# GDN triangular inverse on TensorE: its first four levels as 32 by 32 blocks at four places of the array

## The reference, cut to what matters

```python
lower = jnp.where(strict, jnp.einsum('bhtd,bhsd->bhts', kb, kc) * decay, 0.0)
sol = lax.linalg.triangular_solve(eye + lower, rhs, left_side=True, lower=True, unit_diagonal=True)
u, w = sol[..., :dv], sol[..., dv:]
v_new = u - jnp.einsum('bhcd,bhde->bhce', w, S)
```

## Time and profile before

| what | value |
|---|---|
| median of 3 runs | 1388.18 us (1387.21 to 1388.41) |
| the profiled execution's own time | 1389.42 us |
| its span, first to last instruction | 1387.5 us |
| what lies around the span | 1.92 us |
| PE busy | 1371.8 us, 99% |
| DVE, ACT, POOL busy | 62%, 42%, 25% |
| mean granted TensorE clock | 0.995 |

### The profile page before, as it was taken

One profiled execution on the slowest core, in us unless ns is written; L12 is line 12 of the kernel. 1 busy time (PEld: TensorE's weight loads), 2 busy tenths in 40 slices (PEclk: granted clock), 3 DMA queues, 4 the chain that ended last, 5 costly groups with the idle time before them and its releaser, 6 DMA issues.

```text
span 1387.5 us, 27546 instructions
## 1 busy us (share of the span) xinstructions
PE 1371.8 (99%) x10726; PEld 1335.5 (96%) x10726; DVE 854.1 (62%) x1425; ACT 584.1 (42%) x1061; POOL 352.9 (25%) x478
## 2 busy tenths in 40 slices
PE   8999999999999999999999999999999999999998
PEld 8999999999889999999999999998999799999998
DVE  6666646467676666655766655567663667666542
ACT  6333323434765333332433332367644544333331
POOL 4000013876426000012100002466766340000000
PEclk9999999999999999999999999999999999999999
DMA  7655962334522655854455594143332325555661
GB/s 202 182 148 149 275 173 55 117 115 136 160 69 66 174 148 147 223 159 103 122 151 151 151 251 132 43 121 92 93 93 78 97 82 145 151 151 157 165 163 38
DMA packets 324068, 188.35 MB, mean 136 GB/s; under 512 B 10986, under 2 KB 321384, under 8 KB 323996
## 3 DMA queue, kind: packets, MB, share of 16 engines
q1 hardware_dynamic: 322416, 183.23, 48.2%
q0 software_dynamic: 1216, 3.98, 0.9%
q10 hardware_dynamic: 364, 0.15, 0.1%
HBM read 183.22 MB, written 4.11 MB: 135 GB/s over the span
## 4 chain that ended last, share of the span: by engine, by line
PE 94%; DVE 3%; ACT 2%; issue 1%; DMA 0%; POOL 0%; SPq 0%; DVEq 0%; ACTq 0%
PE PS L677 22%; PE PS L678 22%; PE PS L679 22%; PE PS L794 3%; PE PS L815 2%; PE PS L796 2%; PE PS L795 2%; PE PS L817 2%; PE PS L816 2%; PE PS L767 1%; PE PS L769 1%; PE PS L768 1%; DVE h_lo L2019 1%; PE PS L1258 1%; PE PS L1277 1%; PE PS L1290 1%
## 5 line engine op out<-in xcount | busy, mean ns | idle before, releaser
L677 PE MATMUL PS<-h_hi,w_parts 128*128 128x320 f32 x1408 | 436.6, 310 | 1.8 <-DVE h_lo L2019 1.1
L679 PE MATMUL PS<-h_hi,w_parts 128*128 128x320 f32 x1408 | 435.1, 309 | 0.0
L678 PE MATMUL PS<-h_lo,w_parts 128*128 128x320 f32 x1408 | 435.0, 309 | 0.0
L677 PEld LDWEIGHTS PS<-h_hi,w_parts 128*128 128x128 f32 x1408 | 264.3, 188 | 3.4 <-DVE h_lo L2019 1.7
L678 PEld LDWEIGHTS PS<-h_lo,w_parts 128*128 128x128 f32 x1408 | 264.3, 188 | 0.3
L679 PEld LDWEIGHTS PS<-h_hi,w_parts 128*128 128x128 f32 x1408 | 264.3, 188 | 0.0
L1434 ACT ACTIVATE w_parts<-gu 128x1024 fp32r<-128x1024 f32 (+1 forms) x178 | 176.9, 1041 | 159.8 <-PE PS L679 155.0
L677 PE MATMUL PS<-act_hi,w_parts 128*128 128x320 f32 x704 | 217.7, 309 | 0.0
L679 PE MATMUL PS<-act_hi,w_parts 128*128 128x320 f32 x704 | 217.5, 309 | 0.0
L678 PE MATMUL PS<-act_lo,w_parts 128*128 128x320 f32 x704 | 217.5, 309 | 0.0
L2007 DVE TENSOR_TENSOR w_parts<-gu,w_parts 128x1024 fp32r<-128x1024 f32 x174 | 206.8, 1230 | 4.1 <-ACT w_parts L1434 3.8
(11 more groups left out here) (379 smaller groups left out, 2186.6 us busy)
## 6 DMA issues: line engine op xcount, KB each, us to landing
dn<-in_ffn_w_down SPq DMA_DIRECT2D x32, 1408.0 KB, 7.0
gu<-in_ffn_w_gate SPq DMA_DIRECT2D x87, 512.0 KB, 4.0
gu<-in_ffn_w_up SPq DMA_DIRECT2D x87, 512.0 KB, 5.2
gu<-in_od_w_in SPq DMA_DIRECT2D x32, 512.0 KB, 4.9
gu<-in_ev_w_in SPq DMA_DIRECT2D x26, 512.0 KB, 4.6
dn<-in_ev_w_out SPq DMA_DIRECT2D x4, 1024.0 KB, 5.7
dn<-in_od_w_out SPq DMA_DIRECT2D x4, 1024.0 KB, 5.5
RB<-bias_rows POOLq DMA_DIRECT2D x2, 576.0 KB, 6.1
```

The costliest lines, as they stand in the source:

```text
L677: mm(out, w_hi, hi, start=first, stop=False)
L678: mm(out, w_hi, lo, start=False, stop=False)
L679: return mm(out, w_lo, hi, start=False, stop=last)
```

## The change

The parts y, t and turn of m = 0 to 19 are computed on the 32 by 32 diagonal blocks alone: each of the 4 pairs in 4 blocks of 32 partitions, at four diagonal places of the array, 16 matmuls of 32 by 32 in place of 8 of 64 by 64. The evacuations still read the whole bank regions, so two new memsets on DVE put zeros into banks 4 and 6, with a new semaphore `zeroed`: the first in DVE's step 8, behind `differences(1)`; the second in step 14, behind `first_t(4)`, where it waits for `kt_evac`. `inverse_y(0)` waits for the first, `inverse_t(0)` for the second in place of `kt_evac`. For m = 20 to 24 nothing changes.

```diff
@@ inverse_y, inverse_t, inverse_turn (TensorE)
+            def diagonal_blocks():
+
+                for p in range(C_PAIRS):
+                    for i in range(4):
+                        yield p, slice(32 * i, 32 * i + 32), slice(i % 2 * 32, i % 2 * 32 + 32)
+
             def inverse_y(m):
 
                 c = m % NCH
+                if m == 0:
+                    pe.wait_ge(o["zeroed"], 1)
...
+                if m < 4 * NCH:
+                    for p, rows, w in diagonal_blocks():
+                        ins = mm(by_head(4)[rows, p, w], level[rows, c, p, w], uT[rows, c, p, w], start=True, stop=True)
+                    ins.then_inc(o["y_pe"], 1)
+                    return
...
                 if m:
                     pe.wait_ge(o["t_upd"], m)
                 else:
-                    pe.wait_ge(o["kt_evac"], NCH)
+                    pe.wait_ge(o["zeroed"], 2)
+                if m < 4 * NCH:
+                    for p, rows, w in diagonal_blocks():
+                        ins = mm(by_head(6)[rows, p, w], yT[rows, m % 2, p, w], tT[rows, c, p, w], start=True, stop=True)
+                    ins.then_inc(o["t_pe"], 1)
+                    return
                 for p in range(C_PAIRS):
                     for par in range(2):
                         h = head_rows(par)
-                        left, right = yT[h, m % 2, p, :], tT[h, c, p, :]
-                        if m >= 4 * NCH:
-                            left, right = right, left
-                        ins = mm(by_head(6)[h, p, :], left, right, start=True, stop=True)
+                        ins = mm(by_head(6)[h, p, :], tT[h, c, p, :], yT[h, m % 2, p, :], start=True, stop=True)
...
-                for p in range(C_PAIRS):
-                    for par in range(2):
-                        h = head_rows(par)
-                        ins = mm(by_head(7)[h, p, :], tT[h, m % NCH, p, :], ident[h, h], start=True, stop=True)
+                for p, rows, w in diagonal_blocks():
+                    ins = mm(by_head(7)[rows, p, w], tT[rows, m % NCH, p, w], ident[rows, rows], start=True, stop=True)
                 ins.then_inc(o["u_pe"], 1)
@@ odd (VectorE)
                     if t == 8:
                         differences(1)
+                        ve.wait_ge(o["row_used"], 2)
+                        ve.memset(bank(4)[:, 0:C_PAIRS * CH], 0.0).then_inc(o["zeroed"], 1)
...
                     if 10 <= t < 15:
                         first_t(t - 10)
+                    if t == 14:
+                        ve.wait_ge(o["kt_evac"], NCH)
+                        ve.memset(bank(6)[:, 0:C_PAIRS * CH], 0.0).then_inc(o["zeroed"], 1)
                     if 14 <= t < N_CONV:
                         inverse_update(t - 14)
```

More of the change, by code:

```diff
@@ L517, in build @@
                  "sq qt_pe recip rstd am lev0 kk_pe kk_used kt_evac vt_pe vt_evac t1 u1_pe u1_evac bm y_pe y_evac "
-                 "t_pe u_pe t_upd u_upd cs_pe cs_evac eg qe ks_pe r_ready vn_pe vn_evac o_pe s_pe s_upd osum "
+                 "zeroed t_pe u_pe t_upd u_upd cs_pe cs_evac eg qe ks_pe r_ready vn_pe vn_evac o_pe s_pe s_upd osum "
                  "orecip o_evac decayed turned zt og")
```

## The result

The changed kernel takes 1392.56 us (median of 7 runs, 1390.65 to 1395.61), the kernel before 1388.08 in the same comparison (7 runs, 1387.21 to 1388.41): ratio 1.0033, 95% interval 1.0024 to 1.0043, slower by 0.3%. That is inside the predicted range of 1391 to 1414, on the predicted side, and half of the predicted growth (+4.5 in place of +9.0). The terms of the sum came out otherwise than predicted.

A forecast was written before the change was run, and what follows sets the result against it. PE, busy 99% of the span, was taken to bound the kernel. Terms 3.3 + 1.0 + 3.2 + 1.5 = 9.0 us gave 1398.4 for the profiled execution, 1397.2 us against the median of 1388.18; range 1391 to 1414.

The forecast's parts named there:

- Parts 1 and 2: In y, t and turn: 32 by 32 matmuls, +3.3 us, and nine new array-shape switches between 64 and 32 blocks, +1.0.
- Part 3: In step 14 PE stalls at t(0), waiting for the second memset behind DVE's other work: +3.2 us.
- Part 4: Behind the stall at t(0) PE's clock falls to half, which lengthens the following projection: +1.5 us.
- Part 5: First memset, evacuations and the fetch of 1920 more PE instructions, all costed at nothing.
- Part 1: In y, t and turn, 16 pairs of records take 0.53 us a part against 0.467: +3.3 us over 60 parts.
- rival C: In the parts, records at four places start 10 ns apart, -8.8 us: 1385.1 us in all, faster; chance 0.05.
- A: In the parts, instruction count sets PE's pace, a record keeps its price: 1421.9 us, partly 1405 to 1412; chance 0.25.
- B: The clock also falls in the long runs of parts, steps 24 to 28: +7.5, 1404.7 us; chance 0.17.
- D: No stall at t(0), since DVE comes earlier than read: 1392.5 us, still slower; chance 0.03.

The follow-up runs named there:

- early memset: The changed kernel with the second memset moved on DVE from behind first_t(4) in step 14 to before first_t(3) in step 13: 1386.12 us, ratio 0.9988.
- gaps moved by 16 records: The changed kernel with the second memset in step 13 and first_inverse(4) issued twice, 16 records more ahead of all gaps: 1387.59 us (one run).
- one-place kernel: The changed kernel with a part's 16 matmuls reordered, four in a row at each place, late memset kept: 1404.99 us (one run).
- memsets alone: The kernel before with only the two memsets and their waits added, all matmuls 64 by 64: 1393.76 us, ratio 1.0041.
- two levels: The changed kernel with 32 by 32 blocks only for m = 0 to 9: 1389.82 us with the memset in step 14, 1384.52 in step 13.
- three-level kernel: The changed kernel with 32 by 32 blocks only for m = 0 to 14 and the second memset in step 13: 1383.08 us, ratio 0.9969.

## Why the prediction was right, and where it was wrong

That the time fell into the range, and on the slower side, was luck: two terms missed on opposite sides, the parts by 11.9 us and the fetch by 5.4. With the matmuls as they came out and no gaps, the stretch would have been 2.8 us shorter than before and the kernel faster; it is slower only through a term that was put at nothing. The range held for the same reason: its low end was drawn for pairs at 27 to 30 ns, which did not occur. Predicted and measured in the stretch of the account:

| term | predicted | measured | by |
|---|---|---|---|
| Parts 1 and 2: matmuls and switches | +4.3 | -7.6 | the account; 0.13 us a part in this and three other kernels |
| Part 3: stall at t(0) | +3.2 | +3.3 | the wait; early memset |
| Part 4: half clock behind it | +1.5 | +1.5 | projection 15 |
| Part 5: instruction fetch | 0 | +4.1 gaps, +1.3 half clock | gaps moved by 16 records |
| sum | +9.0 | +2.6 (median +4.5) | |

**Part 1 failed**, in one sentence of it: "four places don't help either while two records of one place stand behind each other". At one place the pair of records does take about what I reckoned, 2 x 19 = 38 ns against 33 to 35. But pairs of other places run beside it, and a part falls to 0.34 us on average (0.53 predicted). The mechanism of rival C, given 0.05, is what happened: starts some 10 ns apart, and -7.6 for parts and switches against its -8.8 + 1.0. I had read the uneven starts of the earlier trace rows as the two records of a matmul in series and two places overlapped. The one-place kernel speaks against that reading: there single starts are 25 to 32 and 4 to 7 ns apart, mostly in turn, although the place stays the same for eight records. So a short step is no sign of a change of place. The averages in the earlier trace rows allow a simpler reading: 29.2 ns a record at 64 columns and 54 at 128 are 0.39 ns a column and some 4 ns for the rest, which at 32 columns is 17 ns, near the 19 of one place. By it quarters of 64 rows would not overlap at all, while 32-row places do; no run put 64 by 64 matmuls at one place to test the first half. Before the run nothing in the trace had 32-row places, so the overlap wasn't to be read; but the bound of -8.8 was, and with it I should have given C far more than 0.05.

The page "TensorE: Matmul & The Clock Gate" of the Trainium skill, section "Back-to-back issue gap", gives an issue floor of about 25 ns for matmuls of 1 to 64 columns. The prediction's estimate from it took each record as a matmul. Counted so, the floor doesn't hold here: 19 ns at one place, 8 to 13 at four. Counted by matmul, two records each, one place with 38 ns is above it, and four places, 16 matmuls in 0.34 us on average or 21 ns each, are below. The about 4 ns between tiles of its Part 3 on packing small matmuls weren't reached as an average either.

**Parts 3 and 4 were right** for the changed kernel, mechanism and size, and the pair of runs with late and early memset confirm them: 1392.56 - 1386.12 = 6.4 and 1389.82 - 1384.52 = 5.3 us (5.5 and 4.5 in the stretch, with gaps that differ by some tenths), against 4.7 predicted. With the memsets alone the half clock cost 3.0 us and not 1.5. The memset took 0.27 us, 0.3 assumed.

**Part 5 failed.** I named the work, "1920 more PE instructions have to be fetched", and costed it at nothing by the queue's share of the DMA engines, 0.3%. It is 0.3% after too. The cost is the delay of a single block at a moment when PE runs through it faster than it comes, and a share can't show that. At the pace of 29 ns there was no gap, neither in the kernel before nor with twice the records in the long runs.

**The rivals.** A is refuted by the parts. B is refuted as put: the clock stays in the runs of parts themselves (1.00 from 1000 to 1040 us and from 1047.5 to 1049.5, in the middle of a run of six); the half clock of 1051 to 1055 follows the gap. C had the right mechanism and the wrong total, since parts and switches gave 7.6 of its 7.8 us and the gaps, with the half clock behind one, took back 5.4. D is refuted by the 3.33.

**Where the levels pay.** With the early memset the median of the four-level kernel falls by 1.8 us, with two levels by 3.4, with three by 5.0: the first 45 parts gain 0.13 each with one gap; the last 15 stand in the long runs of steps 26 to 28, where they gain 2 us and cost two gaps and a half clock.

## What to carry to other kernels

Here small matmuls at different places of the array paid by overlap: with the same 32 columns a part took 0.64 us at one place and 0.34 at four. Measure the distance of starts at one, two and four places before trusting either a floor or a bound. A long run of close instructions can wait for its own instructions, so look for idle times "issue" inside a run of one line. Fewer close parts in the long runs made the gaps fewer here (three, then one); breaking such runs by work whose instructions last was not tried. A memset or other preparation belongs on a step where its engine reaches it before the consumer does; here one step earlier was worth some 5 us, of which the stall was 3.3 and the clock behind it 1.5.

## What was not expected of the hardware

- 32 by 32 records of float32 start 19 ns apart on average at one place, 10 to 13 at two places, 8 to 13 at four, while each still lasts 191 ns, against 218 for 64 by 64:

```profile
L1265 PE MATMUL PS<-RB x640: 184/191/212, 970.3 to 1063.9; 32*32 32x32 f32 x160
```

- Gaps of up to 2.07 us inside runs of close records, at the same numbers of PE's instruction stream in every kernel; PE goes on 2.2 to 2.8 us after a packet of the instruction queue starts. At 19 ns a record one of 0.12 us was left, at 29 ns none.
- After an idle of 2.9 to 3.3 us the half clock lasted 3.4 us in two kernels and 6.8 us in three, the longer where it began 0.6 us or more before PE went on. Idle times of 0.41 to 1.18 us inside the parts left no half clock behind them; those of 1.78 to 2.07 us each did.
- The half clocks don't belong to the program alone. In the profiled execution of the kernel before, the clock fell behind both groups of L1189 rows, the second of them in the earlier trace rows; that of the three-level kernel runs the same matmuls at 1.00 throughout (PE busy, granted clock, DMA share, GB/s):

```profile
925.00:960.00 35.00, 32.60 (x246) 1.00 0.30 91
```
